# First layer of a two-block transformer kernel reordered: loads in parts, norms by chunks, value projections between heads, output projection in two parts

## Chip, cores and metric

One core of one Trainium2 chip. The metric is the device time of one execution in microseconds (us); lower is better.

## What is computed

256 tokens of width 1024, batch 1, in float32, go through two blocks. The first block is one hybrid layer:

```
hn = rms_norm(x, g_mix);  proj = hn @ w_in            # queries, keys, values of 6 dilated and 6 MoBA heads, queries of 4 memory heads
kv = rms_norm(mem, g_memtok) @ w_mem_kv               # keys and values of the memory heads
q, k = rms_norm over each head of 64 columns
o = softmax(q k^T / 8 + bias) v                       # masked with per-head bias; memory heads without
y = concat(rms_norm(o_dil), rms_norm(o_moba), rms_norm(o_mem)) @ w_out;  x = x + y
x = x + peer_ffn(rms_norm(x, g_ffn))                  # 8 heads pick 16 of 128 x 128 single-neuron experts each
```

The second block has two layers: modulated norm, projections, three attention branches of eight heads each (forget gate, latent, stick-breaking), each branch's output projection times a sigmoid gate, their sum through w_out, and a gated FFN of 22 tiles; a final norm ends it. Vectors of modulation come from c_2 and w_ada_2.

## The kernel before

Activations lie transposed: a chunk is 128 features by 256 tokens, eight chunks are the width. Weights stream through a ring of six slots of 512 KB (`ring`), one `dma_start` per slot on SyncE (SP) once an earlier slot is begun (L439 to L444 in the first layer). Each engine has its own written-out order of instructions; semaphores tie them. The first layer goes so:

1. **Loads** (L431 to L437): input `xT`, constants `cst`, vectors `vec`, memory `memT`, early constants, `cond`, positions, all on SP's queue and all counted by one semaphore, `in_loaded`; TensorE, ScalarE and VectorE wait for its full value, 112. Six ring slots follow (L439).
2. **Norms** (`norm`, L1355 to L1364): VectorE squares all eight chunks in one instruction, TensorE sums over features with a ones matrix (`square_sum`, L535), ScalarE takes the root (L982), VectorE the reciprocal (L1361) and scales each chunk (L1364). First the input's, then memory's.
3. **Projections** (`linear`, L509): 14 tiles of 8 matmuls (query and key tiles); then values of the dilated and the MoBA heads with tokens on the partitions (`tokens_major`, L524), then memory's two key tiles and its values. Two PSUM banks take turns, ScalarE evicts (`evict`, L978). Meanwhile VectorE makes the heads' bias, the rotation angles (L1442 to L1468) and eight of the 24 early modulation columns (`modulation_early`, L1438: a product with a 512 KB weight tile that ScalarE's queue fetches in batches of eight, `fetch_early`, L1020).
4. **Pair norms**: for eight pairs of query/key tiles a sum over each head on TensorE (L606), a root on ScalarE (L1042), a reciprocal of 512 columns (L1482) and two scalings (L1486) on VectorE. TensorE waits for all of them.
5. **Heads** (`attention`): 16 heads, six dilated, six MoBA, four of memory (wider, without bias), in a software pipeline: TensorE scores(a) (L550), turn(a-2), a transpose of the probabilities (L562), values(a-3) (L572 to L576); VectorE adds the bias and takes the maximum (L1389, L1384), and divides (L1399, L1405); ScalarE takes exponentials (L993) and copies the turned probabilities (L1003); VectorE takes a finished pair (L1410).
6. **Group norms**: three, one after the other, of 3, 3 and 2 chunks; then the output projection (`mix`, L625), eight tiles into two banks, each added to `xT` by VectorE (L1504), with the second eight modulations between; then the FFN's norm, and the query projection of the PEER stage, 16 tiles (L509 again), the last eight modulations beside it.

The rest of the span is the expert stage and the two layers of the second block. There each weight half-slot is split into a high part by ScalarE (L1067, `weight_high`) and a low part by VectorE (L1739, `weight_low`), and TensorE makes three passes. In each layer 24 branch tiles (three branches of eight) are multiplied by their gate on VectorE (L1892) and summed (L1895). In the third branch ScalarE copies each finished chunk as the high part of the merged sum (L1280, L1284) and VectorE takes the low part (L1886, L1900), in this order:

```
weight_low(LH_WO + jj + 2)
if br == 2 and j:
    v.wait_ge(mhi_chunk, l * DC + j)
    v.tensor_tensor(m_lo[:, j - 1, :], merged[:, j - 1, :], m_hi[:, j - 1, :], ALU.subtract)
```

and on ScalarE `weight_high(LH_WO + h)`, then the copy of chunk h - 18. Before the FFN, VectorE makes the low parts of half-slots 1 and 2 ahead of the norm's reciprocal (L1704) and that of 3 behind it; ScalarE's table for Silu is loaded at L1294.

## Time and profile before

| | us |
|---|---|
| runs | 2370.96, 2366.08, 2369.57 (median 2369.57) |
| profiled execution | 2365.43 |
| its span in the profile | 2363.6 |
| TensorE busy | 2141.9 |
| VectorE busy | 1504.0 |
| ScalarE busy | 993.9 |
| GpSimd busy | 253.0 |
| mean granted TensorE clock | 0.961 |

A line of a timeline gives start, duration, engine, line of the kernel, operation, output and input, count and, in brackets, the idle time before it and what ended it. PE is TensorE's matmuls, PEld its weight loads, DVE VectorE, ACT ScalarE, POOL GpSimd, SPq and ACTq the DMA issues on the queues of SyncE and ScalarE. PEclk is the granted clock of TensorE: 1.00 is 2.4 GHz, 0.50 is 1.2 GHz, and a value between is a window with both. A float32 matmul of 256 columns appears as two records. The tiles in one large buffer are all called arena.

### The profile page before, as it was taken

Reading aid. Unit: us, or ns where it says so; the run is one execution under the profiler, and the core shown is the slowest. Engines: PE = TensorE matmul, PEld = TensorE weight load, DVE = VectorE, ACT = ScalarE, POOL = GpSimd, SP = SyncE. Lnnn points to the kernel's source line nnn. Section 1 sums busy time; section 2 is a strip of 40 time slices with the busy share of each in tenths; the row PEclk is TensorE's granted clock in tenths of the full one; section 3 lists DMA queues with packets and bytes.
Section 4 is the critical chain, followed back from the end, with each engine's and each line's share of the span. In section 5 each row is a group of like instructions: output and inputs, shape, how many; then the busy total and the mean of one; then the engine's idle time right before and its main releaser. Section 6 shows DMA issues by size and latency. Waiting matters only on the chain.

```text
span 2363.6 us, 45897 instructions
## 1 busy us (share of the span) xinstructions
PE 2141.9 (91%) x15318; PEld 1957.5 (83%) x15318; DVE 1504.0 (64%) x3423; ACT 993.9 (42%) x1944; POOL 253.0 (11%) x292
## 2 busy tenths in 40 slices
PE   5948699986799999999998999989998999988998
PEld 4725588875699999999998878878997887878998
DVE  4164419939876777888776446666665536665665
ACT  1023016642344444444445444544444544454444
POOL 0000008989600000000000000000000000000000
PEclk9965899999999999999999999999999999999999
DMA  6420354530155788888763542334553452233553
GB/s 244 160 88 1 107 195 143 169 116 0 48 183 181 249 263 261 267 270 270 264 216 124 177 136 95 110 125 149 183 184 128 161 177 82 95 127 128 186 186 116
DMA packets 102683, 376.14 MB, mean 159 GB/s; under 512 B 11409, under 2 KB 11665, under 8 KB 102049
## 3 DMA queue, kind: packets, MB, share of 16 engines
q1 hardware_dynamic: 88704, 324.23, 40.5%
q10 hardware_dynamic: 13856, 50.40, 6.4%
q8 instruction: 62, 1.02, 0.2%
q14 instruction: 61, 0.49, 0.1%
HBM read 373.54 MB, written 1.05 MB: 158 GB/s over the span
## 4 chain that ended last, share of the span: by engine, by line
PE 52%; issue 21%; DMA 11%; POOL 7%; DVE 4%; DVEq 3%; ACT 1%; ACTq 0%; POOLq 0%; PEldq 0%
PE bank L667 15%; PE bank L673 14%; PE bank L670 14%; DMA roots<-ada_dram 11%; POOL one_hots L1342 5%; POOL part_lo L1331 3%; DVEq L1894 1%; PE bank L805 1%; PE bank L891 1%; ACT part_hi L1067 1%; PE bank L850 1%; PE bank L845 1%; PE bank L847 1%; PE bank L852 1%; PE bank L769 1%
## 5 line engine op out<-in xcount | busy, mean ns | idle before, releaser
L1067 ACT ACTIVATE part_hi<-ring 128x512 fp32r<-128x512 f32 x1080 | 663.6, 627 | 516.4 <-PE bank L670 426.5
L667 PE MATMUL bank<-u_hi,part_hi 128*128 128x256 f32 (+1 forms) x2496 | 722.7, 290 | 54.1 <-DVE u_lo L1712 26.5
L673 PE MATMUL bank<-u_hi,part_lo 128*128 128x256 f32 (+1 forms) x2496 | 706.0, 283 | 0.0
L670 PE MATMUL bank<-u_lo,part_hi 128*128 128x256 f32 (+1 forms) x2496 | 704.0, 282 | 0.0
L1624 DVE TENSOR_TENSOR part_lo<-ring,part_hi 128x512 fp32r<-128x512 f32 x672 | 450.1, 689 | 200.2 <-ACT part_hi L1067 191.1
L667 PEld LDWEIGHTS bank<-u_hi,part_hi 128*128 128x128 f32 (+1 forms) x2496 | 472.7, 189 | 78.3 <-issue 42.1
L673 PEld LDWEIGHTS bank<-u_hi,part_lo 128*128 128x128 f32 (+1 forms) x2496 | 476.8, 191 | 0.5
L670 PEld LDWEIGHTS bank<-u_lo,part_hi 128*128 128x128 f32 (+1 forms) x2496 | 474.5, 190 | 1.0 <-issue 0.5
L667 PE MATMUL bank<-w_hi,part_hi 128*128 128x256 f32 x1376 | 390.2, 284 | 2.4 <-DVE part_lo L1624 1.3
L670 PE MATMUL bank<-w_lo,part_hi 128*128 128x256 f32 x1376 | 388.8, 283 | 0.0
L673 PE MATMUL bank<-w_hi,part_lo 128*128 128x256 f32 x1376 | 388.7, 282 | 0.0
L1739 DVE TENSOR_TENSOR part_lo<-ring,part_hi 128x512 fp32r<-128x512 f32 (+1 forms) x312 | 211.7, 685 | 145.6 <-ACT part_hi L1067 137.7
L667 PEld LDWEIGHTS bank<-w_hi,part_hi 128*128 128x128 f32 x1376 | 262.7, 191 | 5.2 <-DVE part_lo L1624 3.1
L673 PEld LDWEIGHTS bank<-w_hi,part_lo 128*128 128x128 f32 x1376 | 263.0, 191 | 0.0
L670 PEld LDWEIGHTS bank<-w_lo,part_hi 128*128 128x128 f32 x1376 | 263.0, 191 | 0.0
L1331 POOL TENSOR_TENSOR part_lo<-ring,part_hi 128x512 fp32r<-128x512 f32 x96 | 141.2, 1496 | 371.0 <-ACT part_hi L1067 368.1
L978 ACT ACTIVATE arena<-bank 128x256 f32<-128x256 f32 (+2 forms) x176 | 71.1, 410 | 209.3 <-PE bank L509 100.8
L1651 DVE CUSTOM_DVE_ANT_0 roots<-roots,cond 128x1024 f32<-128x1024 f32 x72 | 88.2, 1225 | 68.1 <-DMA roots<-ada_dram 68.1
L1342 POOL TENSOR_SCALAR one_hots<-cst,roots 128x128 f32<-128x128 f32 x192 | 111.6, 610 | 4.7 <-PEq L713 4.3
L509 PE MATMUL bank<-uT,ring 128*128 128x256 f32 x480 | 105.5, 383 | 5.7 <-DVE uT L1364 5.7
L721 PE MATMUL bank<-one_hots 128*128 128x128 f32 x512 | 73.7, 288 | 40.4 <-POOL one_hots L1342 40.4
L509 PEld LDWEIGHTS bank<-uT,ring 128*128 128x128 f32 x480 | 92.2, 192 | 18.9 <-DVE uT L1364 6.1
(253 smaller groups left out, 2482.4 us busy)
## 6 DMA issues: line engine op xcount, KB each, us to landing
ring<-stream_dram SPq DMA_DIRECT2D x606, 512.0 KB, 3.3
roots<-ada_dram ACTq DMA_DIRECT2D x72, 512.0 KB, 4.4
arena<-ada_dram ACTq DMA_DIRECT2D x24, 512.0 KB, 7.5
cst<-consts_dram SPq DMA_DIRECT2D x1, 1097.0 KB, 7.0
xT<-x_dram SPq DMA_DIRECT2D x1, 1024.0 KB, 4.9
arena<-mem_dram SPq DMA_DIRECT2D x1, 1024.0 KB, 9.0
arena<-keys_dram SPq DMA_DIRECT2D x1, 1024.0 KB, 6.1
out_dram<-uT SPq DMA_DIRECT2D x2, 512.0 KB, 2.6
```

Of the source, the lines that this page charges most:

```text
L509: m = pe.matmul(b[0:width, 0:S], w[:, c * width:(c + 1) * width], src[:, c, :], start=c == 0, stop=c == kc - 1)
L667: m = pe.matmul(o, hi, u(cc), start=first, stop=False, **flags)
L670: m = pe.matmul(o, hi, l(cc), start=False, stop=False, **flags)
L673: m = pe.matmul(o, lo, u(cc), start=False, stop=last, **flags)
L721: m = pe.matmul(bank[q][:, t * P:(t + 1) * P], hot_j[:, x, :], hot_i[:, x, :], start=True, stop=True)
L978: return act.activation(dst, src, func, scale=scale, bias=bias).then_inc(tile_out, 1)
L1067: act.activation(part_hi[:, h % 4, 0:width], ring[:, n % RING, (h % 2) * width:(h % 2 + 1) * width], ACT.Copy).then_inc(hi_ready, 1)
L1331: pool.tensor_tensor(part_lo[:, h % 4, :], ring[:, n % RING, (h % 2) * 512:(h % 2 + 1) * 512], part_hi[:, h % 4, :], ALU.subtract).then_in ...
L1342: m = pool.tensor_scalar(hot_j[:, q * 4 + t, :], cst[:, C_IOTA:C_IOTA + P], pickT[:, 1, it * 8 + q * 4 + t:it * 8 + q * 4 + t + 1], None, ...
L1624: v.tensor_tensor(part_lo[:, h % 4, :], ring[:, n % RING, (h % 2) * 512:(h % 2 + 1) * 512], part_hi[:, h % 4, :], ALU.subtract).then_inc(l ...
L1651: v.tensor_tensor_reduce(ada_w, ada_w, cond[:, :], 1.0, 0.0, ALU.mult, ALU.add, ada_col[:, r % 6:r % 6 + 1]).then_inc(ada_used, 1)
L1739: v.tensor_tensor(part_lo[:, h % 4, 0:w], ring[:, slot_of_half(h) % RING, (h % 2) * w:(h % 2 + 1) * w], part_hi[:, h % 4, 0:w], ALU.subtra ...
```

## The change

- **Loads.** The input comes in four loads with a semaphore each. ScalarE's queue loads the first 512 columns of the constants (the ones matrix among them) and the vectors. On SP two ring slots come ahead of memory, four behind it, then the rest, each with its own semaphore. The stream's slots are taken in a new order (`FIRST_ROWS`): queries and keys, memory's keys, dilated values, memory's values, MoBA values.
- **Norms.** ScalarE squares chunk by chunk, TensorE sums each chunk as it comes, and the first tile of a projection takes each scaled chunk as it comes. Memory's norm lies behind the second projection tile. The pair norms run between the projection tiles (pair p behind tile 2p + 3), in banks 6 and 7.
- **Heads.** The order is dilated, memory, MoBA. The ten value slots are projected between heads (`FILL`). The turned probabilities go through bank 4 alone. Pairs are squared by ScalarE as they are taken, and the sums of the first two groups lie between heads 12 and 15, in bank 5. Eight modulations lie between VectorE's heads.
- **Output projection.** All eight banks; the first four tiles take the five chunks of the first two groups, then the three of the last; the squares of the result are made and summed between the last tiles.
- **Query projection.** The angles and the other sixteen modulations lie beside it on VectorE, both Sin and the third batch of loads on ScalarE behind tile 8.
- **Second block.** ScalarE's and VectorE's high and low parts of the merged chunks come one iteration later; half-slot 2's low part of the FFN comes behind the norm. ScalarE's copy is now the helper `merged_high`.

The diff, cut to its core:

```diff
+FIRST_ROWS = [r + j for r, n in ((0, W_IN_QK), (R_MEM_K, MEM_K), (R_V, 4), (R_MEM_K + MEM_K, MEM_V), (R_V + 4, 4))
+              for j in range(n)]
...
+PAIR_CHUNK = (0, 1, 2, 6, 7, 3, 4, 5)
+FILL = {0: ("dil", "dil"), 1: ("dil",), 2: ("dil",), 4: ("mem",), 6: ("mem",),
+        8: ("moba",), 9: ("moba",), 11: ("moba",), 12: ("moba",)}
...
-            sp.dma_start(xT[:, :, :], x_in).then_inc(in_loaded, 16)
-            sp.dma_start(cst[:, :], consts).then_inc(in_loaded, 16)
-            sp.dma_start(vec[:, :], vecs).then_inc(in_loaded, 16)
-            sp.dma_start(memT, mem_in).then_inc(in_loaded, 16)
-            sp.dma_start(erl, early).then_inc(in_loaded, 16)
-            sp.dma_start(cond[:, :], cond_in).then_inc(in_loaded, 16)
-            sp.dma_start(pos_i[:, :], pos_in).then_inc(in_loaded, 16)
-            for s in range(RING):
+            for k in range(4):
+                sp.dma_start(xT[:, 2 * k:2 * k + 2, :], x_in[:, 2 * k:2 * k + 2, :]).then_inc(x_loaded[k], 16)
+            for s in range(2):
                 sp.dma_start(ring[:, s, :], stream[s]).then_inc(loaded[s], 16)
+            sp.dma_start(memT, mem_in).then_inc(mem_loaded, 16)
+            for s in range(2, RING):
+                sp.dma_start(ring[:, s, :], stream[s]).then_inc(loaded[s], 16)
+            sp.dma_start(erl, early).then_inc(early_loaded, 16)
+            sp.dma_start(cst[:, 512:C_KEEP], consts[:, 512:C_KEEP]).then_inc(cst_loaded, 16)
+            sp.dma_start(cond[:, :], cond_in).then_inc(cond_loaded, 16)
+            sp.dma_start(pos_i[:, :], pos_in).then_inc(pos_loaded, 16)
             nfirst = (S_PEER // RING) - 1
-            with sp.Fori(1, 1 + nfirst) as it:
+            for n in range(RING, 5 * RING):
+                sp.wait_ge(slot_begun, n + 2 - RING)
+                row = FIRST_ROWS[n] if n < S_OUT1 else n
+                sp.dma_start(ring[:, n % RING, :], stream[row]).then_inc(loaded[n % RING], 16)
+            with sp.Fori(5, 1 + nfirst) as it:
...
+            pe.wait_ge(ones_loaded, 16)
+            for c in range(DC):
+                pe.wait_ge(x_sq, c + 1)
+                m = sum_squares(bank[2][:, 0:S], c, c == 0, c == DC - 1)
+            m.then_inc(x_sum, 1)
+            for j in range(W_IN_QK + MEM_K):
+                if j == W_IN_QK:
+                    pe.wait_ge(mem_normed, 1)
+                if j < W_IN_QK:
+                    linear(S_QK + j, T_QK + j, uT, DC, fresh=(x_normed, 0) if j == 0 else None)
+                else:
+                    linear(S_QK + j, T_QK + j, memT, DC)
+                if j == 1:
+                    pe.wait_ge(mem_sq, 1)
+                    for c in range(DC):
+                        m = sum_squares(bank[2][:, 0:S], c, c == 0, c == DC - 1)
+                    m.then_inc(mem_sum, 1)
+                if j >= 3 and j % 2:
+                    pair_sum((j - 3) // 2)
...
+            def turn(a):
+                pe.wait_ge(prob_ready, a + 1)
+                if a:
+                    pe.wait_ge(pt_copied, a)
...
+                w = slot(n + k)
+                if k == 0:
+                    pe.wait_ge(tile_out, t)
...
+            pe.wait_ge(pnorm_ready, 4)
+            for a in range(16 + 3):
+                if a == 6:
+                    pe.wait_ge(pnorm_ready, 9)
+                if a < 16:
+                    scores(a)
+                if a == 0:
+                    pair_sum(7)
+                for kind in FILL.get(a, ()):
+                    project_values(kind)
+                if a == 12:
+                    group_sum(bank[5][:, 0:S], (0, 1, 2))
+                if a == 15:
+                    group_sum(bank[5][:, S:2 * S], (3, 4))
+                if 0 <= a - 2 < 16:
+                    turn(a - 2)
+                if 0 <= a - 3:
+                    if a - 3 in (0, 6, 10):
+                        pe.wait_ge(tile_out, {0: T_V, 6: T_MEM_V, 10: T_VM}[a - 3] + 2)
+                    values(a - 3)
+            group_sum(bank[4][:, 0:S], (5, 6, 7))
...
+            def mix_part(j, chunks, first, last):
+                w = slot(S_OUT1 + j)
+                for i, c in enumerate(chunks):
+                    if j == 0:
+                        pe.wait_ge(og_chunk, PAIR_CHUNK.index(c) + 1)
+                    m = pe.matmul(bank[j][:, 0:S], w[:, c * P:(c + 1) * P], oT[:, c, :],
+                                  start=first and i == 0, stop=last and i == len(chunks) - 1)
+                    if i == 0 and last:
+                        m.then_inc(slot_begun, 1)
+                if last:
+                    m.then_inc(mix_full, 1)
...
+            pe.wait_ge(score_read, 16)
+            for j in range(4):
+                mix_part(j, PAIR_CHUNK[0:5], True, False)
+            for j in range(4):
+                mix_part(j, PAIR_CHUNK[5:8], False, True)
+            for j in range(4, 8):
+                mix_part(j, PAIR_CHUNK, True, True)
+                for c in {4: (), 5: (0, 1), 6: (2, 3), 7: (4, 5)}[j]:
+                    mixed_sum(c)
+            mixed_sum(6)
+            mixed_sum(7)
             for j in range(PEER_Q):
-                linear(S_PQ + j, T_PQ + j, uT, DC)
+                linear(S_PQ + j, T_PQ + j, uT, DC, fresh=(p_normed, 0) if j == 0 else None)
...
+            act.dma_start(cst[:, 0:512], consts[:, 0:512]).then_inc(ones_loaded, 16)
+            act.dma_start(vec[:, :], vecs).then_inc(vec_loaded, 16)
+            act.preload_act_table(ACT.Sqrt)
+            for c in range(DC):
+                if c % 2 == 0:
+                    act.wait_ge(x_loaded[c // 2], 16)
+                square(sq[:, c, :], xT[:, c, :]).then_inc(x_sq, 1)
...
+            for j in range(W_IN_QK + MEM_K):
+                evict(T_QK + j, qk[:, j, :])
+                if j == 1:
+                    act.wait_ge(mem_sum, 1)
+                    root_of(wgt2[:, 0, :], bank[2][:, 0:S]).then_inc(mem_root, 1)
+                    act.wait_ge(cond_loaded, 16)
+                    act.activation(cond[:, :], cond[:, :], ACT.Silu).then_inc(cond_ready, 1)
+                if j == 2:
+                    fetch_early(0)
+                if j >= 3 and j % 2:
+                    pair_root((j - 3) // 2)
+            pair_root(7)
...
+            def square_pair(p):
+                act.wait_ge(out_taken, p + 1)
+                square(sq[:, p, :], oT[:, PAIR_CHUNK[p], :], 1.0).then_inc(og_sq, 1)
+
+            for a in range(16 + 2):
+                if a in (3, 7, 13):
+                    t, v, width = {3: (T_V, v_dil, 384), 7: (T_MEM_V, v_mem, 256), 13: (T_VM, v_moba, 384)}[a]
+                    for tt in range(2):
+                        evict(t + tt, v[:, tt, :], width=width)
+                if a < 16:
+                    exps(a)
+                if a == 15:
+                    act.preload_act_table(ACT.Sqrt)
+                if a >= 2:
+                    copy(a - 2)
+                if a >= 6 and a % 2 == 0:
+                    square_pair((a - 6) // 2)
+                if a == 12:
+                    fetch_early(1)
+                if a == 16:
+                    act.wait_ge(og_sum, 2)
+                    root_of(root[:, 0:S], bank[5][:, 0:S], 1.0 / 384).then_inc(og_root, 1)
+                    root_of(root[:, S:2 * S], bank[5][:, S:2 * S], 1.0 / 256).then_inc(og_root, 1)
+            square_pair(6)
+            square_pair(7)
+            act.wait_ge(og_sum, 3)
+            root_of(wgt2[:, 0, :], bank[4][:, 0:S], 1.0 / 384).then_inc(og_root, 1)
...
             for j in range(PEER_Q):
                 evict(T_PQ + j, qry[:, j, :])
+                if j == 8:
+                    act.wait_ge(turn_ready, 1)
+                    act.activation(cosT[:, :], tab[:, 0, :], ACT.Sin)
+                    act.activation(sinT[:, :], tab[:, 1, :], ACT.Sin).then_inc(rope_ready, 1)
+                    fetch_early(2)
...
                 for h in range(9, 24):
                     weight_high(LH_WO + h)
-                    if h >= 18:
-                        c = h - 18
-                        act.wait_ge(merged_ready, l * DC + (c + 1))
-                        act.activation(m_hi[:, c, :], merged[:, c, :], ACT.Copy).then_inc(mhi_chunk, 1)
-                for c in (6, 7):
-                    weight_high(LH_OUT + c - 6)
-                    act.wait_ge(merged_ready, l * DC + (c + 1))
-                    act.activation(m_hi[:, c, :], merged[:, c, :], ACT.Copy).then_inc(mhi_chunk, 1)
+                    if h >= 19:
+                        merged_high(h - 19)
+                for c in (5, 6, 7):
+                    if c < 7:
+                        weight_high(LH_OUT + c - 5)
+                    merged_high(c)
...
+            v.wait_ge(early_loaded, 16)
+            v.wait_ge(cst_loaded, 16)
+            for p in range(9):
+                if p < 8:
+                    v.wait_ge(tile_out, T_QK + 2 * p + 2)
+                    pair = qk[:, 2 * p:2 * p + 2, :].rearrange("p a b -> p (a b)")
+                    v.tensor_tensor(pairsq[:, p, :], pair, pair, ALU.mult).then_inc(psq_ready, 1)
+                if p == 0:
+                    v.wait_ge(mem_root, 1)
+                    v.reciprocal(wgt2[:, 1, :], wgt2[:, 0, :])
+                    v.drain()
+                    for c in range(DC):
+                        m = v.scalar_tensor_tensor(memT[:, c, :], memT[:, c, :], vec[:, V_GMEM + c:V_GMEM + c + 1],
+                                                   wgt2[:, 1, :], ALU.mult, ALU.mult)
+                    m.then_inc(mem_normed, 1)
...
+                if p >= 1:
+                    v.wait_ge(proot_ready, p)
+                    v.reciprocal(rstd[:, :], root[:, :]).then_inc(pnorm_ready, 1)
+                    v.drain()
+                    for j in range(2):
...
+            v.drain().then_inc(pnorm_ready, 1)
...
+            for a in range(16 + 4):
+                if a < 16:
+                    top(a)
+                if 0 <= a - 1 < 16:
+                    normalise(a - 1)
+                if a >= 5 and a % 2:
+                    take((a - 5) // 2)
+                if 2 <= a < 10:
+                    modulation_early(a - 2)
...
+            for g, (r, src, pairs) in enumerate(((rstd[:, 0:S], root[:, 0:S], (0, 1, 2)),
+                                                 (rstd[:, S:2 * S], root[:, S:2 * S], (3, 4)),
+                                                 (wgt2[:, 1, :], wgt2[:, 0, :], (5, 6, 7)))):
+                v.wait_ge(og_root, g + 1)
+                v.reciprocal(r, src)
+                v.drain()
+                group_normed(r, pairs)
+            for j in range(M_OUT1):
+                v.wait_ge(mix_full, j + 1)
+                v.tensor_tensor(xT[:, j, :], bank[j][:, 0:S], xT[:, j, :], ALU.add).then_inc(mix_taken, 1)
+            v.wait_ge(p_root, 1)
+            v.reciprocal(rstd[:, 0:S], root[:, 0:S])
...
-            for n in range(8):
-                modulation_early(n)
-            for lo, n in ((0, 3), (6, 3), (12, 2)):
...
-            for n in range(16, 24):
+            for n in range(8, 24):
...
+                def merged_low(c):
+                    v.wait_ge(mhi_chunk, l * DC + (c + 1))
+                    v.tensor_tensor(m_lo[:, c, :], merged[:, c, :], m_hi[:, c, :], ALU.subtract)\
+                        .then_inc(mlo_chunk, 1)
+
                 weight_low(LH_WO + 1)
                 for jj in range(24):
                     br, j = jj // 8, jj % 8
                     weight_low(LH_WO + jj + 2)
-                    if br == 2 and j:
-                        v.wait_ge(mhi_chunk, l * DC + j)
-                        v.tensor_tensor(m_lo[:, j - 1, :], merged[:, j - 1, :], m_hi[:, j - 1, :], ALU.subtract)\
-                            .then_inc(mlo_chunk, 1)
+                    if br == 2 and j >= 2:
+                        merged_low(j - 2)
                     v.wait_ge(mix_full, mixed + (M_OUT1 + jj + 1))
                     if j == 0:
                         v.wait_ge(gate_ready, l * 3 + (br + 1))
...
-                v.wait_ge(mhi_chunk, l * DC + DC)
-                v.tensor_tensor(m_lo[:, DC - 1, :], merged[:, DC - 1, :], m_hi[:, DC - 1, :], ALU.subtract)\
-                    .then_inc(mlo_chunk, 1)
+                merged_low(DC - 2)
+                merged_low(DC - 1)
 
                 def add_out(j):
                     v.wait_ge(mix_full, mixed + (M_OUT1 + 24 + j + 1))
...
-                for h in (1, 2):
+                weight_low(LH_FFN + 1)
+                normed_chunks(l * L_WIDE + 2, wide + DC, lambda c: gm[:, 8 + c:9 + c], lambda c: vec[:, 24 + c:25 + c])
+                for h in (2, 3):
                     weight_low(LH_FFN + h)
-                normed_chunks(l * L_WIDE + 2, wide + DC, lambda c: gm[:, 8 + c:9 + c], lambda c: vec[:, 24 + c:25 + c])
-                weight_low(LH_FFN + 3)
```

## Rows read from the trace of the kernel before

**Rows 1.** The page, part 1: busy us (share of the span) xinstructions.

```profile
PE 2141.9 (91%) x15318; PEld 1957.5 (83%) x15318; DVE 1504.0 (64%) x3423; ACT 993.9 (42%) x1944; POOL 253.0 (11%) x292
```

**Rows 2.** 10 us windows: length, busy (x), granted clock, DMA share, GB/s.

```profile
140.00:150.00 10.00, 5.24 (x6) 1.50 (x6) 9.59 (x8) 1.38 (x2) 0.00 (x0) 0.50 0.00 0
...
180.00:190.00 10.00, 10.00 (x29) 5.52 (x29) 4.78 (x29) 3.56 (x14) 0.00 (x0) 0.50 0.01 2
```

**Rows 3.** Page, part 6 (first line), and timeline (start us, us, engine, line), 0 to 45 us.

```profile
xT<-x_dram SPq DMA_DIRECT2D x1, 1024.0 KB, 4.9
...
16.26 5.92 PE L535 MATMUL bank<-sq,cst 128*128 128x256 f32 x16 [16.26 <-DVE sq L1355]
...
24.07 1.75 DVE L1361 RECIPROCAL roots<-roots 128x256 f32<-128x256 f32 x1 [7.95 <-ACT roots L982]
...
36.55 8.80 PE L509 MATMUL bank<-uT,ring 128*128 128x256 f32 x40
```

**Rows 4.** Timeline, 80 to 124 us: values and the first two pair sums.

```profile
85.62 10.56 PE L524 MATMUL bank<-ring,uT 128*128 128x384 f32 x32 [0.56 <-ACT arena L978]
...
116.17 7.14 PE L524 MATMUL bank<-ring,arena 128*128 128x256 f32 x32 [0.56 <-ACT arena L978]
...
123.16 1.88 PE L606 MATMUL bank<-arena,cst 128*128 128x512 f32 x4
```

**Rows 5.** Groups by line, 0 to 330 us: busy us, mean ns.

```profile
L1482 DVE RECIPROCAL roots<-roots 128x512 f32<-128x512 f32 x8 | 26.8, 3354 | 15.2 <-ACT roots L1042 14.8
```

**Rows 6.** Timeline, 165 to 220 us: scores (L550) and first values (L572).

```profile
165.69 1.66 PE L550 MATMUL bank<-arena 64*128 64x128 f32 x8 [10.05 <-DVE roots L1482]
...
173.42 1.11 PE L572 MATMUL bank<-arena 128*64 128x256 f32 x2
...
174.89 1.65 PE L550 MATMUL bank<-arena 64*128 64x128 f32 x4
...
219.07 2.07 PE L550 MATMUL bank<-arena 64*128 64x256 f32 x4
```

**Rows 7.** 4 us windows, columns as in rows 2.

```profile
280.00:284.00 4.00, 0.93 (x3) 0.81 (x4) 2.92 (x3) 0.00 (x0) 0.00 (x0) 0.95 0.00 0
284.00:288.00 4.00, 4.00 (x13) 3.26 (x12) 0.00 (x0) 0.00 (x0) 0.00 (x0) 0.62 0.00 0
...
1548.00:1552.00 4.00, 1.92 (x14) 1.73 (x15) 2.81 (x8) 0.94 (x2) 0.00 (x0) 1.00 0.25 98
```

**Rows 8.** Timeline, 227 to 260 us: last heads taken, output projection, its additions.

```profile
228.77 0.42 DVE L1410 COPY arena<-bank 128x256 f32<-128x256 f32 x1 [1.93 <-PE bank L574]
...
249.46 29.57 PE L625 MATMUL bank<-arena,ring 128*128 128x256 f32 x128 [3.38 <-DVEq L1498]
...
254.89 0.42 DVE L1504 TENSOR_TENSOR xT<-bank,xT 128x256 f32<-128x256 f32 x1 [5.57 <-PE bank L625]
...
258.35 0.42 DVE L1504 TENSOR_TENSOR xT<-bank,xT 128x256 f32<-128x256 f32 x1 [1.89 <-PE bank L625]
```

**Rows 9.** Timeline, 288 to 295 us: eight loads issued on ScalarE's queue, query projection.

```profile
288.52 4.19 ACTq L1020 DMA_DIRECT2D arena<-ada_dram  x8
...
294.16 6.10 PE L509 MATMUL bank<-uT,ring 128*128 128x256 f32 x20 [5.68 <-DVE uT L1364]
```

**Rows 10.** Timeline of VectorE, 1540 to 1564 us: the gate multiplies L1892.

```profile
1540.38 0.42 DVE L1892 TENSOR_TENSOR arena<-bank,arena 128x256 f32<-128x256 f32 x1
...
1542.07 0.42 DVE L1892 TENSOR_TENSOR arena<-bank,arena 128x256 f32<-128x256 f32 x1
...
1545.46 0.42 DVE L1892 TENSOR_TENSOR arena<-bank,arena 128x256 f32<-128x256 f32 x1
...
1563.11 0.42 DVE L1892 TENSOR_TENSOR arena<-bank,arena 128x256 f32<-128x256 f32 x1
```

**Rows 11.** Timeline, 1593 to 1597 us: behind the FFN norm's root.

```profile
1593.91 1.28 ACT L1294 ACT_TABLE_LOAD   x1
...
1596.47 1.75 DVE L1704 RECIPROCAL roots<-roots 128x256 f32<-128x256 f32 x1
```

459 lines of the change are left out of this document (197 added, 262 removed).

## Prediction

> **What bounds the kernel now.** I read the page first: one core, TensorE busy for 91% of the span [rows 1], so time can only be won where TensorE waits or is clocked down. The 10 us windows then show where that is: nearly all of it lies in the first 300 us. The stretch from 140 to 150 us has half of TensorE busy and all of VectorE; that from 180 to 190 has TensorE full, but at a granted clock of 0.50, which is 1.2 GHz, not 2.4 [rows 2]. The timeline of these 300 us gives four losses. (a) Everything waits for one semaphore of seven loads, then the input's norm and memory's norm run one after the other: the first projection starts at 36.55 [rows 3]. (b) Projections and values run densely to about 124, then eight pair norms follow, one reciprocal of 3.35 us each on VectorE [rows 5], and the first head starts at 165.69 [rows 6]. (c) The heads run to 228.8 with the clock at half [rows 2, 6]. (d) Three group norms, the output projection and the next norm run one after the other, and the query projection starts at 294.16 [rows 8, 9]. From there on nothing of the first layer is left to wait for but VectorE's own start of the top-16 stage, which begins when the keys' tiles are out; it moves with the rest.
>
> **The sum, as a new timeline of the first layer.**
> *Front.* The input alone needs 4.9 us from issue to landing for 1 MB [rows 3]; four quarter loads and the ones matrix from ScalarE's queue end at about 5 to 6 us. The squares are now ScalarE's, chunk by chunk, under the arriving loads. The eight sums took 5.92 us from a cold start [rows 3]; I keep that. Then a root of 0.5, the reciprocal of 1.75 [rows 3] and one scaled chunk of 0.4: the first projection starts at about 5 + 5.9 + 2.9 = 13.8 us, against 36.55. Memory's norm and its 3.45 us sum lie between projections; the loads of constants and early bias are needed only by the bias work at about 20 us. That is 22.8 us gained; bounds 19 (input and ring slots share the queue) to 25.
> *Projections.* A tile costs 3.46 us (the step between two outputs in the same stream of eight matmuls) [rows 8]. Sixteen (14 and memory's two keys) are 55.3; memory's sum 3.5; seven pair sums at 0.94 (1.88 for two) [rows 4] 6.6; a start at half clock 2. The first head's scores come at 13.8 + 67.4 = 81 us. The pair norms cost VectorE 3.35 + about 2 a pair, under two tiles and a sum, 7.8 us: hidden. The last two are not: VectorE starts on the heads at about 88, but TensorE has four value slots to do meanwhile (10.56 us in all) [rows 4]. ScalarE also issues eight early loads behind tile 2; a batch takes 4.2 us [rows 9], less than the two free tiles allow.
> *Heads.* From the fifth to the last head the scores come 4.02 us apart (44.18 over eleven steps) at half clock with TensorE full [rows 6, 2]; at full clock 2.01, for 16 heads 32.2. Filling in are the values, 10.56 twice and 7.14 [rows 4], 28.3; a pair sum 0.9; five chunks of group sums 2.2. That is 63.6 of TensorE. VectorE has about 2 us a head plus eight modulations of 1.2, so it doesn't bound. Stalls: 4 where the last values wait for their eviction, which stands on ScalarE behind a second batch of eight DMA issues (4.2) [rows 9], and 4 in the last heads' chain, together 8. So 81 + 63.6 + 8 = 153 if the clock stays.
> *The clock* is the open price. It fell behind the window of 280 to 284, in which TensorE had 0.93 of 4 us busy: 0.95 granted there, 0.62 in the next [rows 7]. I expect the 4 us stall before head 13's values to do the same; what follows (three scores, five turns, six values, sums) is then at half clock: 6 us more, 159. In the other direction, the 1548 to 1552 window has 1.92 us busy of 4 and stays at 1.00 [rows 7], so short gaps alone don't cost it; the fills are dense, so earlier heads keep it.
> *From the last value to the query projection* took 228.77 to 294.16, 65.4 us [rows 8, 9]. Now two group norms are done beneath the heads and five eighths of the first four outputs precede the third. First mix matmul 3.6 after the last value; eight tiles 27.7; sums of squares between them 2.6 and a wait for the third group 1; the first tile took 5.43 instead of 3.46 [rows 8], so 2.0 for the clock, as today; then add, square, two sums, root, reciprocal, one chunk: 4.8. That is 41.7: the query projection starts at 200.5 instead of 294.2, **94 us earlier**.
> *Query projection.* The angles (8 us) and sixteen modulations of 1.2 now lie on VectorE beneath it: 28 of 55 us, and the last batch of loads, issued behind tile 8, has over 20 us to land. But the Sin table load of 1.28, two Sins and eight issues of 4.2 [rows 9, 11] stand on ScalarE before tile 9's eviction: 6.3 us against 6.9 that two tiles give: I take 1 us, bounds 0 and 3. The SP queue's order of loads changes, not their number, and no ring slot is asked for faster than 1.3 us apart.
> *Second block, twice.* In the third branch VectorE's multiplies come 2.94 us apart (17.65 over six) because the next low half waits for the merged chunk of the iteration just ended; in the second branch they come 1.69 apart [rows 10]. With the high part one iteration later the wait is covered and VectorE bounds: 1.69 plus 0.33 for the low part, 2.02. Seven steps of 0.9 are 6 us; lower bound 3 if one ScalarE wait stays. In front of the FFN norm, the reciprocal starts at 1596.47, 2.6 us after the root, behind a table load and a low half [rows 11]; now at once. What is late next is half 2 for the up projection: 0.5. So 2.1. Together 8.1 a layer, **16 us**; bounds 6 and 18.
> *Sum:* 94 - 1 + 16 = 109. The profiled execution took 2365.4 us (its span and 1.8 around it); 2365.4 - 109 = 2256. The median of the three runs shown is 2369.6, 4 over that execution, so the median that I state is 2260.
>
> **A rule against it.** The 180 to 190 window has TensorE always busy with heads and never granted more than 0.50 [rows 2], although dense projections bring it to 1.0 within the first tile [rows 8]. So head work as such does not earn the clock, and heads between two fills could lose it. The Trainium skill, TensorE: Matmul & The Clock Gate, Part 4 (PE-mode transpose), says that a transpose does not count as busy for the clock gate in the way a matmul does. By that rule the trace agrees, but no row here has heads mixed with dense fp32 fills in the first layer.
>
> **Rivals**, as profiled executions (4 more as medians).
> (1) *Forecast*, clock lost only behind the 4 us stall: 2256. Chance 0.45.
> (2) *The clock holds throughout*, because the stall is shorter (for: 1548 to 1552; against: 280 to 284): 6 and 2 us less, 2248. Chance 0.22.
> (3) *Heads at half clock between fills.* For: 180 to 190. Against: the fills. All heads at half cost 32 more, of which 6 are counted and 4 vanish in stalls; five groups of fills each begin slow, 2 us: about 30 more, 2286. Chance 0.20; half of it, 2271, is as well in this case.
> (4) *The second block's moves do not pay*, since the wait was for something else (the change then doesn't do there what it is made for): 12 to 16 lost, 2270. Chance 0.09.
> (5) *Slower.* The turned probabilities have one bank where there were two; turn(a) waits for copy(a-1), and copy stands on ScalarE behind the exponentials of two heads later. If that made heads go one at a time, each would cost what the first does from scores to values, 165.69 to 174.5, 8.8 us [rows 6]; 16 of them 141, plus fills at half clock 57: 198 where I have 78. That is 2376. It decides from 117 us more than I have for this stretch (the 109 and 8 for noise). Against: the loop runs over two heads, and its parts sum to about 5 us per two. Chance 0.02 that it or the like makes it slower, 0.02 that it only eats all.
>
> **How the numbers follow.** The likeliest case gives 2260 as a median. Case (2) with a front at its better bound is 2248 - 2 + 4, and cheaper stalls reach 2242; case (3) is 2290 as a median, and I end at 2292; outside lies between 0.1 and 0.2. About 0.2% is what a measurement of this kernel can tell from no change. Faster 0.97 (cases 1 to 4), same 0.01, slower 0.02.
>
> **What would show it.** The first projection at 12 to 16 us; the first scores at 78 to 85; window clocks of 1.0 from 90 to 135 and 0.5 just after; one TensorE gap of about 4 us before head 13; the query projection at 195 to 205; VectorE's third-branch multiplies 2.0 us apart. Clock 0.5 between 95 and 135 means case (3); 2.9 us apart means (4); scores more than 8 us apart means (5). A first projection after 20 us, or a TensorE wait on a ring slot, would mean that the loads were mis-sized.

## The result, and where the time went

The changed kernel takes 2254.49 us in the median of four runs (2247.47 to 2255.86), where the kernel before takes 2369.4: a ratio of 0.951, 95% interval 0.9489 to 0.953. The profiled execution took 2255.86 us, with a span of 2254.1. The forecast was a median of 2260 and a profiled execution of 2256.

TensorE's busy time fell by 30 us of the 109.5 us that the span lost (first row of the page, beside [rows 1]); the rest is waits that are gone.

```profile
PE 2112.1 (94%) x15318; PEld 1945.4 (86%) x15318; DVE 1494.1 (66%) x3417; ACT 1004.8 (45%) x1976; POOL 252.3 (11%) x292
```

TensorE's waits in the first 260 us of the changed kernel, without one of 0.5 (columns: waited for, us in total, times, longest):

```profile
PE bank L545 <- DVE uT L1465: 6.2, 2, 3.2
PE bank L568 <- ACT sq L1054: 5.5, 1, 5.5
PE bank L684 <- DVE arena L1465: 2.6, 2, 1.4
PE bank L623 <- ACT arena L1051: 2.5, 1, 2.5
```

Seventeen microseconds are left there: the two norms' last steps (3.2 and 3.0), the loading of the input, two short waits for normed chunks, and one stall in the heads. The timeline of TensorE has the milestones that answer to [rows 3, 6, 8, 9]:

```profile
14.02 7.15 PE L545 MATMUL bank<-uT,ring 128*128 128x256 f32 x32 [3.18 <-DVE uT L1465]
...
139.64 1.12 PE L623 MATMUL bank<-arena 128*64 128x256 f32 x2 [2.47 <-ACT arena L1051]
...
154.25 0.38 PE L627 MATMUL bank<-arena 128*64 128x128 f32 x2
...
157.46 1.53 PE L684 MATMUL bank<-arena,ring 128*128 128x256 f32 x6 [1.16 <-DVE arena L1465]
160.38 19.69 PE L684 MATMUL bank<-arena,ring 128*128 128x256 f32 x90 [1.39 <-DVE arena L1465]
...
193.43 8.91 PE L545 MATMUL bank<-uT,ring 128*128 128x256 f32 x33 [3.00 <-DVE uT L1465]
...
261.44 0.55 PE L740 MATMUL bank<-u_hi,part_hi 128*128 128x256 f32 x1 [2.88 <-POOL part_lo L1441]
```

The first of these expert matmuls and the first norm of the second block were, in the kernel before:

```profile
362.16 0.55 PE L667 MATMUL bank<-u_hi,part_hi 128*128 128x256 f32 x1 [2.88 <-POOL part_lo L1331]
...
1250.97 1.74 DVE L1704 RECIPROCAL roots<-roots 128x256 f32<-128x256 f32 x1
```

and the four norms of the second block in the changed kernel's timeline of VectorE:

```profile
1159.95 1.75 DVE L1808 RECIPROCAL roots<-roots 128x256 f32<-128x256 f32 x1
...
1496.97 1.75 DVE L1808 RECIPROCAL roots<-roots 128x256 f32<-128x256 f32 x1 [0.89 <-ACT roots L1247]
...
1704.73 1.75 DVE L1808 RECIPROCAL roots<-roots 128x256 f32<-128x256 f32 x1
...
2042.37 1.75 DVE L1808 RECIPROCAL roots<-roots 128x256 f32<-128x256 f32 x1 [0.89 <-ACT roots L1247]
```

| stretch of the profiled execution | before | after | gain |
|---|---|---|---|
| start to first projection | 36.55 | 14.02 | 22.5 |
| to the query projection | 257.61 | 179.41 | 78.2 |
| to the first expert matmul | 68.00 | 68.01 | 0.0 |
| to the second block's first norm | 888.81 | 898.51 | -9.7 |
| to its FFN norm | 345.50 | 337.02 | 8.5 |
| to the next layer's norm | 209.68 | 207.76 | 1.9 |
| to its FFN norm | 346.06 | 337.64 | 8.4 |
| to the end | 211.39 | 211.73 | -0.3 |

The sum is 109.5. Two lines are not among the change's steps. **The expert stage** runs for 400 us at 256 to 271 GB/s (part 2 of the page, slices of 56 us), and TensorE waits now and then for VectorE, which waits for a load, as here (timeline of the changed kernel, VectorE, then TensorE):

```profile
1112.87 1.23 DVE L1755 CUSTOM_DVE_ANT_0 roots<-roots,cond 128x1024 f32<-128x1024 f32 x1 [3.29 <-DMA roots<-ada_dram]
...
1114.77 0.58 PE L740 MATMUL bank<-u_hi,part_hi 128*128 128x256 f32 x1 [2.17 <-DVE part_lo L1728]
```

The stage took 888.8 us in this profile of the kernel before, 898.5 in this one, and 891.7 to 901.7 in the eleven other profiles of the changed first layer below. With the old first layer and the second block's edits it took 892.9. The place of the difference can be read: VectorE's 72 products with loaded tiles (L1651 before, L1755 now) begin 420.7 us behind the first expert matmul in the kernel before and 420.6 in the changed one, and the last begins at 843.0 and at 851.4. So 8.5 of the 9.7 us lie in the stretch that loads feed, and the twelve profiles of a changed first layer scatter there by 10 us among themselves. Whether the change slows it a little besides is not shown: the two profiles with the old first layer, 888.8 and 892.9, are both in the lower half, where the twelve others have a mean of 895.4. The medians differ by 115, the profiles by 109.5; the profile of before was 4 us under its median, that of the changed kernel 1.4 above its own. **The 1.9 us** is told of at the end.

### The profile page after: what moved, and what is told of

It is laid out like the page before. It is cut to its first block, busy times and chain, and to the rows that moved or that the text cites. A ratio compares the mean times of both kernels' runs of the same rounds, so it can differ in the third digit from the quotient of the medians.

```text
span 2254.1 us, 45848 instructions
## 1 busy us (share of the span) xinstructions
PE 2112.1 (94%) x15318; PEld 1945.4 (86%) x15318; DVE 1494.1 (66%) x3417; ACT 1004.8 (45%) x1976; POOL 252.3 (11%) x292
## 4 chain that ended last, share of the span: by engine, by line
PE 56%; issue 17%; DMA 10%; POOL 8%; DVE 4%; DVEq 3%; ACT 1%; ACTq 0%; POOLq 0%; PEldq 0%
PE bank L740 16%; PE bank L746 15%; PE bank L743 15%; DMA roots<-ada_dram 10%; POOL one_hots L1452 5%; POOL part_lo L1441 3%; DVEq L2002 1%; PE bank L878 1%; PE bank L964 1%; DVE part_lo L1728 1%; PE bank L918 1%; PE bank L923 1%; PE bank L925 1%; PE bank L920 1%; PE bank L842 1%
## 5 line engine op out<-in xcount | busy, mean ns | idle before, releaser
L1755 DVE CUSTOM_DVE_ANT_0 roots<-roots,cond 128x1024 f32<-128x1024 f32 x72 | 88.2, 1225 | 77.1 <-DMA roots<-ada_dram 76.9
## 6 DMA issues: line engine op xcount, KB each, us to landing
cst<-consts_dram SPq DMA_DIRECT2D x1, 841.0 KB, 14.3
```

The source lines that it names most:

```text
L1755: v.tensor_tensor_reduce(ada_w, ada_w, cond[:, :], 1.0, 0.0, ALU.mult, ALU.add, ada_col[:, r % 6:r % 6 + 1]).then_inc(ada_used, 1)
```

## The experiments

All times are compared with the changed kernel unless said otherwise. Whole runs of one kernel scatter by 3 to 15 us, and beside these experiments the kernel before took 2371.4 to 2372.1 in the median, not 2369.4; so I read the stretch that an edit touches, in one profile of each kernel. For the first layer that is from the first projection to the query projection, 179.4 us in the changed kernel.

**1. The stall before head 13, and the clock.** In the changed kernel eight issues of early loads stand on ScalarE's queue ahead of the eviction that the values of head 10 wait for (TensorE makes them in the same round as the scores of head 13). Timeline of ScalarE, then 4 us windows (columns as in [rows 2]):

```profile
134.89 0.82 ACTq L1079 DMA_DIRECT2D arena<-ada_dram  x2
...
135.74 2.94 ACTq L1079 DMA_DIRECT2D arena<-ada_dram  x6
138.72 0.87 ACT L1051 ACTIVATE arena<-bank 128x384 f32<-128x384 f32 x2 [3.05 <-issue]
```

```profile
132.00:136.00 4.00, 4.00 (x19) 2.60 (x18) 0.08 (x1) 1.20 (x4) 0.00 (x0) 1.00 0.49 139
136.00:140.00 4.00, 1.53 (x8) 0.89 (x8) 1.75 (x10) 1.28 (x5) 0.00 (x0) 0.82 0.94 351
140.00:144.00 4.00, 4.00 (x12) 2.17 (x11) 1.02 (x8) 1.09 (x4) 0.00 (x0) 0.50 1.02 415
...
152.00:156.00 4.00, 4.00 (x21) 2.58 (x19) 1.76 (x3) 2.36 (x7) 0.00 (x0) 0.97 0.02 4
```

```diff
-                if a == 12:
-                    fetch_early(1)
...
             root_of(wgt2[:, 0, :], bank[4][:, 0:S], 1.0 / 384).then_inc(og_root, 1)
+            fetch_early(1)
```

> Compared with the changed kernel (2254.5 us median, last head's values issued at 154.25, query projection from 193.43). One edit: ScalarE issues the second batch of eight early loads behind the third group's root, not between heads 12 and 13. (A) My theory: the 2.47 us gap of TensorE at 139.6, made by those issues ahead of the eviction of the values, drops the clock, and everything from there to 152 runs at half. Then the gap shrinks under 1 us, the 4 us windows from 136 to 152 are granted 1.0, the last values come at 147 to 149, the query projection at 186 to 189, and the time falls 5 to 7 us to about 2248.5. (B) Rival: the last heads are too thin to keep the clock whatever the gap. Then only the gap comes back, 2.5 us: clock 0.5 from about 140 to 152, last values at about 152, query projection at 191. (C) Rival: the copy of turned probabilities or VectorE is late next and nothing comes back: 193.

Measured: 2246.22 us (2245.03 to 2252.78), ratio to before 0.9477 (0.9457 to 0.9497). The stall is gone; what is left is this wait, in which a turn waits until ScalarE, behind a table load, has copied the bank of the turn before, with these windows:

```profile
148.94 0.52 PE L613 MATMUL bank<-cst,arena 128*128 128x128 f32 x3 [1.73 <-ACT arena L1118]
```

```profile
144.00:148.00 4.00, 3.21 (x17) 2.05 (x15) 2.62 (x14) 3.12 (x9) 0.00 (x0) 1.00 0.00 0
148.00:152.00 4.00, 3.06 (x15) 2.06 (x16) 0.42 (x1) 3.06 (x8) 0.00 (x0) 0.80 0.02 6
```

Up to 148 us the clock stays at 1.00, with TensorE busy 3.2 of 4 us, so (B), heads too thin to keep it, falls. The query projection came at 191.87, not 186 to 189, because in this execution the first two tiles ran at half clock, 10.04 us instead of 7.15. From the first projection it is 177.1, less those 2.9: 174.2, which is 5.2 better than 179.4. (A) holds for the stall, at the low end; its windows of 1.0 up to 152 and its gap under 1 us did not come, as the clock fell behind the 1.73 us wait (0.80 from 148, 0.78 in the window from 152).

**2. Do the value projections between the heads hold the clock?**

```diff
-FILL = {0: ("dil", "dil"), 1: ("dil",), 2: ("dil",), 4: ("mem",), 6: ("mem",),
-        8: ("moba",), 9: ("moba",), 11: ("moba",), 12: ("moba",)}
+FILL = {0: ("dil",) * 4 + ("mem",) * 2 + ("moba",) * 4}
...
+            for t, v, width in ((T_V, v_dil, 384), (T_MEM_V, v_mem, 256), (T_VM, v_moba, 384)):
+                for tt in range(2):
+                    evict(t + tt, v[:, tt, :], width=width)
             for a in range(16 + 2):
...
```

> Compared with the changed kernel. All ten value slots are projected and evicted behind the first head's scores, none between heads. (A) The fills hold the clock in the heads, as my forecast had it: without them the granted clock falls to 0.50 within a few heads, as it did in the 180 to 190 window of the kernel before; heads come about 4.0 us apart; last values at 79 + 29 of values + 16 times 4 = 170 to 178 instead of 154.25; the time rises 15 to 24 us to 2270 to 2278. (B) Rival: a TensorE that waits only briefly between heads keeps its clock, and half clock in the kernel before came from how its heads began. Then heads are 2.0 to 2.9 us apart (VectorE's work on a head, 2, and 1.2 for a modulation), clock 1.0, last values at 148 to 156, time within 4 us of 2254.5.

Measured: 2272.68 us (2262.58 to 2277.68). The matmul at which VectorE was late, what ScalarE did ahead of it, and windows:

```profile
118.51 0.55 PE L612 MATMUL bank<-cst,arena 128*128 128x128 f32 x3 [3.22 <-DVE arena L1546]
...
115.35 1.28 ACT L1107 ACT_TABLE_LOAD   x1
116.64 0.40 ACT L1107 ACTIVATE arena<-arena,small 128x128 f32<-128x128 f32 x1
```

```profile
116.00:120.00 4.00, 1.49 (x7) 0.83 (x7) 2.26 (x14) 3.18 (x12) 0.00 (x0) 0.95 0.00 0
120.00:124.00 4.00, 3.30 (x11) 2.16 (x11) 3.60 (x13) 2.03 (x8) 0.00 (x0) 0.50 0.00 0
...
152.00:156.00 4.00, 4.00 (x17) 1.96 (x15) 1.59 (x11) 1.87 (x8) 0.00 (x0) 0.79 0.00 0
156.00:160.00 4.00, 4.00 (x21) 2.76 (x20) 1.88 (x11) 2.59 (x9) 0.00 (x0) 1.00 0.10 13
...
168.00:172.00 4.00, 2.27 (x14) 1.36 (x12) 1.42 (x6) 3.27 (x8) 0.00 (x0) 1.00 0.62 250
```

The stretch to the query projection is 15.5 us longer (197.7 less 2.9 for its own slow start, against 179.4), as (A) had it; its first heads come 3.9 us apart at half clock. But its reason is only half right. The clock fell behind one wait of 3.2 us, then came back at 154 in the midst of heads, with no dense projection near, and stayed at 1.00 in windows with TensorE busy 2.27 of 4 us. So heads can earn the clock and keep it without fills between them.

The wait itself is in good part the edit's own. It moved all evictions of the values ahead of the first exponentials, and the first of these had its maximum at 93.2 but ran at 116.64, behind the last eviction (114.46) and a table load. So the run doesn't show what fills between the heads are worth: no run has the fills ahead of the heads without that wait, and the 15.5 us are the price of this order as a whole.

The trace of the kernel before has the same return of the clock, which I had overlooked:

```profile
220.00:224.00 4.00, 4.00 (x11) 1.80 (x9) 2.57 (x9) 1.23 (x5) 0.00 (x0) 0.50 0.00 0
224.00:228.00 4.00, 4.00 (x19) 2.46 (x19) 1.10 (x4) 1.92 (x4) 0.00 (x0) 0.80 0.00 0
```

It rose at 225.6, 60 us after the first head and 20 us after the first scores of a memory head; in experiment 2 it rose at 153.7, 34 us after it fell and 23 us after the first scores of a memory head. In both, the memory heads with their wider matmuls had run just before. In the changed kernel it rose at 152.2 among MoBA heads, 14 us after its fall. What brings it back is open.

The Trainium skill (TensorE: Matmul & The Clock Gate, Part 4, PE-mode transpose), which the prediction sets against itself, says that full clock does not engage for transposes. The windows from 156 on, where every head has its three or four turns, do not bear it out as a rule for a mix with matmuls; no run here has transposes alone.

**3. The front's loads.** Squares of the input wait for all loads.

```diff
+            for s in (vec_loaded, mem_loaded, early_loaded, cst_loaded, cond_loaded, pos_loaded):
+                act.wait_ge(s, 16)
             for c in range(DC):
```

> Compared with the changed kernel. ScalarE's first square of the input waits for every load of the front (all landed at about 23.4 us by the records) instead of the first quarter of the input; the order of the loads and of the norms stays. (A) The single semaphore was the larger part of the front: first projection at 23.4 + 0.4 + 5.5 + 2.9 = 32 instead of 14.0, and the whole kernel 18 us later, about 2272. (B) Rival: the larger part was that the two norms ran one after the other, and loads would have been there in any case: then the first projection is at 22 or earlier and the time at most 8 us up. (C) Rival: a later start is absorbed by the pair norms or by a wait for ring slots: first projection at 32, query projection less than 14 later.

Measured: 2271.14 us (2265.62 to 2271.78). First projection at 32.70, 18.7 later, as (A) says. Of the 22.5 us won at the front, 18.7 belong to not waiting for all loads, which leaves 3.8 for the order of the two norms and the squares on ScalarE. This run had the same stall in the heads, and the clock did not fall:

```profile
158.36 0.65 PE L623 MATMUL bank<-arena 128*64 128x256 f32 x2 [2.51 <-ACT arena L1051]
```

```profile
156.00:160.00 4.00, 1.64 (x8) 0.98 (x8) 1.18 (x7) 2.12 (x7) 0.00 (x0) 1.00 1.01 404
160.00:164.00 4.00, 4.00 (x21) 2.47 (x20) 3.01 (x19) 2.48 (x10) 0.00 (x0) 1.00 1.03 421
```

So its first to query projection took 175.6 us, 3.8 less than 179.4: this is what the clock alone is worth behind that stall, by one execution.

**4. Pair norms.** Seven pair sums on TensorE and their roots on ScalarE stand behind the sixteen projections.

```diff
-                if j >= 3 and j % 2:
-                    pair_sum((j - 3) // 2)
+            for p in range(7):
+                pair_sum(p)
```

> Compared with the changed kernel. The sums and roots of the first seven pair norms stand behind the sixteen projections, as in the kernel before, not between them. (A) VectorE's pair norms are then bare: 5.2 us each in the kernel before, here 6 with the squares of the next pair; scores of the first head behind six of them at about 73 + 36 = 109 instead of 78.91, VectorE's start on the heads at about 121 instead of 88, with four value slots beneath it. The query projection comes 30 to 34 us later, time 2283 to 2290. (B) Rival: the fills make up for it, since TensorE has 63 us of work in the heads and VectorE less: under 20 us.

Measured: 2282.17 us (2280.05 to 2283.65). The pair sums come about 6 us apart, at half clock, each waiting for VectorE; the second of them:

```profile
84.85 2.08 PE L574 MATMUL bank<-arena,cst 128*128 128x512 f32 x2 [5.89 <-DVE arena L1485]
```

The stretch is 213.1 long, less 3.0 for its slow start 210.1: 30.7 more. (A) holds. This is the largest term of the first layer that an experiment takes out by itself.

**5. Group norms and the output projection.** First both undone (all sums and roots behind the last head, one wait for all eight chunks), then only the wait.

```diff
...
+            pe.wait_ge(og_chunk, 8)
             for j in range(4):
                 mix_part(j, PAIR_CHUNK[0:5], True, False)
...
```

> Compared with the changed kernel. All three groups' sums, roots and norms of the first layer's heads stand behind the last head, and the output projection starts when all three are done. (A) Both parts were needed: five sums of 0.38 us and two roots come first, then reciprocals of 1.75 three times and eight chunks of 0.4 on VectorE: normed at about 154.6 + 1.9 + 1.2 + 1 + 8.6 = 166.5 where the first mix matmul of the changed kernel came at 157.46; TensorE idles 8 us, the query projection comes 9 to 10 us later plus up to 2 for the clock, time 2263 to 2266. (B) Rival: the wait for the third group, 1.39 us of idle, hid the same chain already: under 3 us.

> Compared with the changed kernel. The group sums and norms stay beneath the heads, but the output projection's first matmul waits until all eight chunks are normed, so the projection in two parts has nothing to fill. (A) The chunks are done at 163.7 by the records (the third reciprocal at 160.64 + 1.75 and three chunks of 0.4), 6.2 us after 157.46; of that the 1.39 us wait goes, so the query projection is 4.9 us later, up to 2 more for the clock, time 2259 to 2261. (B) Rival: VectorE is done sooner than that without the competition: under 2 us.

Measured: 2263.57 us (2261.67 to 2265.06) for both, 2258.78 (2254.77 to 2261.48) for the wait alone. The first mix matmul, in the one and in the other:

```profile
168.53 23.73 PE L682 MATMUL bank<-arena,ring 128*128 128x256 f32 x96 [8.20 <-DVE arena L1463]
```

```profile
163.96 22.51 PE L684 MATMUL bank<-arena,ring 128*128 128x256 f32 x96 [7.65 <-DVE arena L1466]
```

The stretch is 190.7 and 185.1 long: 11.3 and 5.7 more. So the projection in two parts is worth 5.7, and group norms beneath the heads another 5.6. Both runs agree with (A). Part of it is the clock: behind the waits it was 0.50 from 164 to 172 in the first, and 0.53 and 0.61 from 160 to 168 in the second.

Experiments 3, 4 and 5 together take back 60.7 of the 100.7 us by which the query projection came earlier. The rest has no experiment of its own. By the records, 16 of it lie in the heads: they took 63.1 us at half clock in the kernel before, with 28.3 of values ahead of them, and take 75.3 now with these values between them.

**6. The second block.** The change has three edits there. I undid one at a time: VectorE's low half one iteration earlier, ScalarE's high half one iteration earlier, and half 2 ahead of the FFN norm.

```diff
-                    if br == 2 and j >= 2:
-                        merged_low(j - 2)
+                    if br == 2 and j:
+                        merged_low(j - 1)
...
```

> Compared with the changed kernel. In the second block's third branch the low half of the merged chunk is again taken one iteration after its sum, not two. (A) My theory: the wait for ScalarE's high half is all of the difference, so the multiplies come 2.9 us apart where they are 2.04 now, 6.3 us in each of the two layers, time about 2267 (+12.6). (B) Rival: the pitch is set by the weights' high and low halves, and what was gained there came from elsewhere: pitch 2.0 to 2.2, time within 3 us of 2254.5.

```diff
-                    if h >= 19:
-                        merged_high(h - 19)
+                    if h >= 18:
+                        merged_high(h - 18)
...
```

> Compared with the changed kernel. In the third branch ScalarE copies the merged chunk's high part in the same iteration again, so that its split of the next weight half stands behind that chunk's sum; VectorE's low part stays where the change put it. The run with only VectorE's part undone kept the pitch of 2.04 us. (A) ScalarE's order is the whole of it: VectorE's multiplies come 2.9 us apart in six of seven steps, the third branch takes 6.3 us more in each layer, +12.6 over the span. (B) Rival: both had to be late together before, and either edit alone is enough: pitch 2.0 to 2.2, time unchanged.

```diff
-                weight_low(LH_FFN + 1)
+                for h in (1, 2):
+                    weight_low(LH_FFN + h)
...
```

> Compared with the changed kernel. VectorE takes the low halves 1 and 2 of the FFN's weights ahead of the FFN norm, as the kernel before did, not half 1 alone. (A) Theory: the reciprocal waits for half 2, whose high part stands on ScalarE behind the root, so it starts 3.4 us after the last output chunk's sum instead of 2.3: by the records 1591.64 to 1596.47 (4.83) before and 1494.69 to 1496.97 (2.28) after; the 2.55 come back in each layer, +5 us over the span, of which up to 1 is hidden because half 2 is then ready: 4 to 5. (B) Rival: the table load makes that distance and the halves are hidden: 2.3 again, time unchanged within 1 us by the records of the layers.

VectorE's multiplies in the third branch of the changed kernel are 2.04 us apart (answering to [rows 10]), and with ScalarE's edit undone 2.88:

```profile
1456.41 0.42 DVE L2000 TENSOR_TENSOR arena<-bank,arena 128x256 f32<-128x256 f32 x1
...
1458.45 0.42 DVE L2000 TENSOR_TENSOR arena<-bank,arena 128x256 f32<-128x256 f32 x1
```

```profile
1457.51 0.69 DVE L1842 TENSOR_TENSOR part_lo<-ring,part_hi 128x512 fp32r<-128x512 f32 x1 [1.00 <-ACT part_hi L1174]
...
1458.45 0.42 DVE L1999 TENSOR_TENSOR arena<-bank,arena 128x256 f32<-128x256 f32 x1
...
1461.34 0.41 DVE L1999 TENSOR_TENSOR arena<-bank,arena 128x256 f32<-128x256 f32 x1
```

- VectorE's edit undone: 2253.44 us (2243.25 to 2255.61), pitch 2.05. My theory fell here: alone this edit is worth 0.4 us a layer at most.
- ScalarE's undone: 2262.89 (2260.54 to 2265.7), pitch 2.88; norm to FFN norm takes 342.6 and 342.3 us in the two layers, 5.6 and 4.6 more. The wait is that for the weight's high part (the row with 1.00): ScalarE cannot split the next half before it has the chunk whose sum VectorE is about to make.
- Half 2 undone: 2258.23 (2255.26 to 2260.8). The reciprocal waits for half 2, whose high part stands behind ScalarE's table load:

```profile
1498.90 0.69 DVE L1843 TENSOR_TENSOR part_lo<-ring,part_hi 128x512 fp32r<-128x512 f32 x1 [2.83 <-ACT part_hi L1174]
1499.51 1.75 DVE L1808 RECIPROCAL roots<-roots 128x256 f32<-128x256 f32 x1
```

It is 2.54 us later in each layer (1469.02 to 1499.51 from the last multiply, 27.95 in the changed kernel), of which 0.2 to 0.3 are hidden.

The two edits make up 14.9 of the 16.9 us. The other 2 may come from undoing both orders together: from the last multiply of the second branch to the last of the third it is 20.5 us in the kernel before, 19.8 with ScalarE's edit undone, 14.7 with VectorE's undone and 14.3 in the changed kernel. No run has both undone.

Then the three edits alone, in the kernel before (the diff is that of the change for these functions):

> The kernel before with the change's edits of the second block alone (high and low parts of the merged chunks one iteration later, half 2 behind the FFN norm). (A) The second block's term stands by itself: 2.9 falls to 2.04 us a step in the third branch, the reciprocal starts 2.3 us behind the last output chunk instead of 4.8, 8 to 9 us in each layer, 16 to 18 us over the span: ratio to the kernel before 0.9925 to 0.9935, about 2354. (B) Rival: part of it shows only together with the first layer's edits: under 10 us. Its expert stage also tells whether 888.8 us from the first expert matmul to the next layer's first norm, as in the profile of the kernel before, is usual there: all profiled runs of the changed first layer took 892 to 902. (C) If the first layer's edits slowed that stage, it is 886 to 890 here again; (D) if the stage scatters by itself, it is anywhere from 888 to 902.

Measured: 2354.87 us (2351.68 to 2360.45), ratio to the kernel before 0.9933 (0.9911 to 0.9954). Norm to FFN norm takes 336.4 us in both layers, 9.1 and 9.6 less. The term stands by itself, as (A) says. The expert stage took 892.9, outside the 886 to 890 of (C) and within (D).

**7. A version faster than the changed kernel.** Experiment 1's edit, and the output projection by groups: ScalarE takes two groups' roots behind the last exponentials, VectorE the first reciprocal between the last heads, and TensorE starts with the first group's three chunks.

```diff
-            for j in range(4):
-                mix_part(j, PAIR_CHUNK[0:5], True, False)
+            mix_part(0, PAIR_CHUNK[0:3], True, False)
+            group_sum(bank[4][:, 0:S], (5, 6, 7))
+            for j in range(1, 4):
+                mix_part(j, PAIR_CHUNK[0:3], True, False)
+            for j in range(4):
+                mix_part(j, PAIR_CHUNK[3:5], False, False)
```

> The changed kernel with the early loads behind the third root (as in the first run), the first two groups' roots right behind the last exponentials, VectorE's first reciprocal between the last heads, and the output projection's first four tiles in three parts, one for each group, the first ahead of the third group's sum. (A) The 2.35 us in which TensorE waits for normed chunks (0.96 and 1.39) vanish, and the third group's reciprocal starts 2 to 3 us earlier than 159.07: from the last head's values to the query projection 2 to 3 us less than the 39.4 there, time 2 to 3 us under the first run's 2246.2. (B) Rival: the reciprocal ahead of the take of the seventh pair delays the third group by as much (0.7 us or more), and what is gained is under 1 us.

Then with added matmuls that only fill two gaps:

```diff
+            def keep_warm(b, n):
+                for _ in range(n):
+                    pe.matmul(bank[b][:, 0:S], ONES, cst[:, 0:S], start=True, stop=True)
...
             m.then_inc(x_sum, 1)
+            keep_warm(3, 8)
...
             mixed_sum(7)
+            keep_warm(5, 7)
```

> The kernel of e8_mix_by_groups with added work on TensorE whose results nobody reads: 8 matmuls of the ones matrix (3.0 us at full clock) between the input's sums and the first projection, 7 (2.7 us) ahead of the query projection, where TensorE was idle 3.18 and 3.00 us. (A) The gaps are what costs the clock behind them: with the fill the granted clock stays at 1.0 from 12 to 28 us and from 192 to 200; the first two tiles of projection take 7.1 us in every run (10.0 where the clock fell), the query projection's first tile 3.5 instead of about 5.4; 2 us less than e8 where its first tiles ran fast, 5 less where they didn't. (B) Rival: the clock there falls from the warm-up of the first microseconds, whatever fills the gap; then time as e8, or 0.5 us more.

Measured: 2244.59 us (2240.54 to 2252.68), ratio 0.9468 (0.944 to 0.9495), and with the filled gaps 2242.11 (2234.73 to 2245.8), ratio 0.9454 (0.9428 to 0.9479). The query projection of the first, then the fills (L572) and projections of the second:

```profile
184.10 31.10 PE L545 MATMUL bank<-uT,ring 128*128 128x256 f32 x143 [3.00 <-DVE uT L1466]
```

```profile
11.32 3.62 PE L572 MATMUL bank<-cst 128*128 128x256 f32 x16
...
182.84 3.19 PE L572 MATMUL bank<-cst 128*128 128x256 f32 x14
186.01 24.20 PE L545 MATMUL bank<-uT,ring 128*128 128x256 f32 x111
```

By groups, TensorE waits for no normed chunk, and the stretch is 170.1, 4.1 under experiment 1's 174.2 (part of it since the clock held behind the 1.73 us wait here and not there). The time is 1.6 us under that run's, within its scatter. With the filled gaps the clock is at 1.00 in every window from 8 to 36 and from 180 to 208. But so it is in the profile of the first kernel, whose gaps are empty, so this pair doesn't show that the fills keep it. For them speaks only that the empty gaps lost it in five of eleven profiles at the front, and in nine of eleven ahead of the query projection. That the fills shorten the whole, by 2.5 us of medians, the intervals do not settle. Against the changed kernel the last version is some 12 us faster, and the intervals of the ratios (0.9428 to 0.9479, and 0.9489 to 0.953) do not meet.

## Why the prediction was right

**Front.** 13.8 forecast, 14.02 measured; the gain 22.8 against 22.5. The squares follow the arriving quarters (the last two from 8.51), and the sums run beneath them from 5.50 to 10.84, where I had 5 to 10.9.

**Projections.** First scores at 78.91, not 81. The 2 us for a start at half clock were not paid in this execution. In five of the eleven profiles of a changed first layer with that gap unfilled they were, and cost 1.5 to 3.0.

**Heads.** 75.3 us from first scores to last value, where I had 78. The stall was 2.47, not 4: ScalarE began its issues at 134.89, while TensorE had work until 137.2. The 4 us of stalls in the last heads' chain did not show. Where these heads ran faster, 1.73 us of them did (experiments 1 and 7). In the heads the clock fell behind the stall and only there; all windows from 80 to 136 are at 1.00. So the mechanism was right, with its price at 3.8 (experiment 3) to 5.2 with the stall (experiment 1), where I had 6 for the clock and 4 for the stall.

**Last value to query projection.** 39.2 us against 41.7; the 2.0 that I took for the clock at the mix's start was the wrong term, as the clock came back at 152, before the mix. It fell one step later, behind the 3.00 us wait (0.65 in the window from 192): the query projection's first tile was evicted 5.29 us behind its start, and 3.73 in experiment 7's first kernel, where it held. So the clock cost 1.6 there. The 2.0 was the difference of a first tile's 5.43 from a step of 3.46 [rows 8], and a first tile takes 3.73 even at full clock.

**Query projection.** 1 us was set aside for the Sin table ahead of tile 9's eviction; 68.01 against 68.00 says zero. The evictions come 3.45 apart up to 226.34, then at 230.24 and 233.25, and TensorE does not wait.

Together the query projection came 100.7 us earlier, not 94.

**Second block.** 16.9 by the norms against 16. The pitch is 2.04 (2.02 forecast), the reciprocal 2.55 earlier (2.6). The prediction named the high part's delay as what covers the wait, which was right; before the experiment I had come to credit VectorE's edit instead, and that was wrong. By single edits ScalarE's order is worth 10.2 and half 2 about 4.7 over two layers.

**The total.** 109.5 between the profiles against 109 is luck: the first layer gave 7.7 more than forecast, the second block 0.9 more, the layer's end 1.9, and the expert stage took back 9.7 that no step had. Between medians the change is worth 115, and my 2260 was 5.5 too slow. I had added 4 for the distance of the shown profile from its median; the other profile lay 1.4 on the other side.

**The rivals.** (2), the clock holds throughout: it fell, though experiment 3 shows that it need not. (3), half clock between fills: false, by the windows. Its premise, that head work as such does not earn the clock, was already against the trace of the kernel before, where it rose to 0.80 and 1.00 from 224 on, within the last heads; and the prediction's "the heads run to 228.8 with the clock at half" is off by these 3 us. (4), the second block does not pay: false. (5), one bank for turned probabilities makes heads go one at a time: no wait of TensorE for it stands in the changed kernel's list of waits. The 1.73 us wait of experiments 1 and 7 is of this kind, once.
